# High parts of the projection's input made by ScalarE from the residual stream, and a re-ordered first stage

## What is computed

```python
for l in range(DEPTH):                                  # DEPTH = 2
    cond = silu(c) @ w_ada[l] + b_ada[l]                # 3 x 1024 values
    shift, scale, gate_raw = split(cond, 3)
    h = x * (1.0 + scale) + shift                       # conditioning of the residual stream
    proj = h @ w_in[l]                                  # 33 tiles of 128 columns, and more
    ...                                                 # two scans, merge
    x = layer_norm(DN_ALPHA * x + (1.0 + gate_raw) * out, ln_g[l], ln_b[l])
```

## Time and profile before

| what | value |
|---|---|
| median of three runs | 4421.1 us (4419.56 to 4424.52) |
| the profiled execution's own time | 4417.15 us |
| its span, first to last instruction | 4415.4 us |
| mean granted TensorE clock | 0.919 |
| TensorE busy (weight loads) | 87% (65%) |
| VectorE, ScalarE, GpSimd busy | 53%, 40%, 25% |
| conditioning | 0 to 48.2 us of the span |
| layer 0's projection, first VectorE instruction | 49.03 us |
| layer 1's projection, first VectorE instruction | 1348.48 us |

### The profile page before, as it was taken

How to read it: one execution, slowest core, us unless ns; L and a number is a source line. 1 busy time by engine, 2 the same in 40 slices (tenths; PEclk the granted TensorE clock), 3 DMA queues, 4 the chain that set the end, 5 groups by cost and what they waited for, 6 DMA issues and landing times. The chain is left out here.

```text
span 4415.4 us, 78502 instructions
## 1 busy us (share of the span) xinstructions
PE 3835.2 (87%) x30764; PEld 2891.4 (65%) x30764; DVE 2356.1 (53%) x2943; ACT 1780.8 (40%) x2347; POOL 1097.6 (25%) x963
## 2 busy tenths in 40 slices
PE   6999888888896999978997988888787999999953
PEld 3888676666674887756665754545555777777733
DVE  3365554553663001834554752752356788878857
ACT  1111245442332111444442332542215777777734
POOL 2221213211332221221221320001004444444424
PEclk8999899888998999988988999998798999999975
DMA  6766324112333432333113412511208888898867
GB/s 216 233 223 194 124 86 151 65 51 83 129 100 109 139 124 78 119 117 110 58 44 121 137 67 96 240 41 39 109 38 333 325 305 323 307 391 354 305 219 257
DMA packets 285206, 724.13 MB, mean 164 GB/s; under 512 B 36112, under 2 KB 127888, under 8 KB 268048
## 3 DMA queue, kind: packets, MB, share of 16 engines
q1 hardware_dynamic: 223600, 392.07, 26.0%
q0 software_dynamic: 48960, 283.17, 16.9%
q10 hardware_dynamic: 12384, 45.09, 2.6%
HBM read 631.09 MB, written 168.82 MB: 181 GB/s over the span
## 5 line engine op out<-in xcount | busy, mean ns | idle before, releaser
L471 PE MATMUL ps<-s_proj_hS,s_proj_wS 128*128 128x512 f32 x3216 | 766.7, 401 | 63.2 <-POOL s_proj_wS L361 63.2
L471 PEld LDWEIGHTS ps<-s_proj_hS,s_proj_wS 128*128 128x128 f32 x3216 | 613.7, 191 | 212.2 <-ACT s_proj_wS L421 64.1
L3365 PE MATMUL ps<-s_exp_wS,exp_x 128*128 128x512 f32 x2208 | 539.1, 399 | 0.0
L3365 PEld LDWEIGHTS ps<-s_exp_wS,exp_x 128*128 128x128 f32 x2208 | 408.8, 189 | 92.8
L526 PE MATMUL ps<-gate_h,gate_w 128*128 128x512 f32 x1536 | 417.7, 424 | 37.2 <-PEq L154 19.3
L513 POOL TENSOR_TENSOR gate_w<-gate_raw,gate_w 128x512 fp32r<-128x512 f32 x128 | 187.4, 1467 | 824.0 <-ACT gate_w L507 823.2
L526 PEld LDWEIGHTS ps<-gate_h,gate_w 128*128 128x128 f32 x1536 | 296.0, 197 | 140.2 <-issue 52.1
L389 DVE COPY s_proj_o<-ps 128x512 f32<-128x512 f32 x66 | 45.6, 691 | 567.6 <-PE ps L471 567.6
L3303 DVE TENSOR_TENSOR s_exp_wS<-exp_gu,s_exp_wS 128x1024 fp32r<-128x1024 f32 x276 | 325.3, 1219 | 29.6 <-ACT s_exp_wS L3249 29.6
L361 POOL TENSOR_TENSOR s_proj_wS<-s_proj_w,s_proj_wS 128x1024 fp32r<-128x1024 f32 x67 | 169.0, 2525 | 567.6 <-ACT s_proj_wS L421 567.6
L3249 ACT ACTIVATE s_exp_wS<-exp_gu 128x1024 fp32r<-128x1024 f32 x276 | 286.6, 1071 | 27.0 <-DMA exp_gu<-in_w_gu_dram,s_exp_widx 16.6
(11 more groups left out here) (487 smaller groups left out, 7050.2 us busy)
## 6 DMA issues: line engine op xcount, KB each, us to landing
yrow<-keep_hT SPq DMA_DIRECT2D x92, 512.0 KB, 4.3
keep_mix<-in_w_ada_dram SPq DMA_DIRECT2D x80, 512.0 KB, 7.1
s_proj_w<-in_w_in_dram SPq DMA_DIRECT2D x66, 512.0 KB, 4.3
proj<-s_proj_o ACTq DMA_DIRECT2D x66, 512.0 KB, 2.7
gate_raw<-in_w_in_dram SPq DMA_DIRECT2D x128, 256.0 KB, 3.2
yrow<-keep_xT SPq DMA_DIRECT2D x4, 8192.0 KB, 49.1
s_rw_edge<-proj SPq DMA_DIRECT2D x34, 512.0 KB, 4.9
s_mix_sg<-gates SPq DMA_DIRECT2D x32, 512.0 KB, 3.3
```

Source lines behind the costliest of these rows:

```text
L471: mm = pe.matmul(k.ps[:, 6 + half if last else 2 * b + half, :], wS[:, b, x, t, :], hS[:, y, t, half * HALF:(half + 1) * HALF], start=(t = ...
L3365: mm = pe.matmul(k.ps[:, 2 if u % 2 == 0 else 6, :], xS[:, u % 2, h, 2 * pr + t, :], wS[:, pr, w, t, :], start=(pr == 0 and t == 0 and h + ...
```

## The change

In conditioning, the weights get four buffers, and SP asks for all four groups at once, then for the eight pieces of the residual stream, and waits for these itself at its end; ScalarE issues nothing. The fourth group is no longer multiplied by TensorE against three vectors. VectorE multiplies its rows by the first vector's value of each partition and adds up over the eight slices (`acc`), and TensorE sums over the partitions by products with ones. The bias is added for the first vector alone, which is the only one that this stage's outputs need.

In the projection, ScalarE makes the high part of each piece from `keep_xT` itself, with `1 + scale` and `shift` as scale and bias for each partition. VectorE computes the same piece into `s_proj_o` (two buffers) and makes all eight remainders; GpSimd has none left and begins with the weights. ScalarE makes the first weight tile's high part after the third piece.

```diff
@@ -172,10 +172,11 @@
     NS = 2 * KT
     NG = NS // GRP
     with Stage(k, "ada") as s:
-        w = s.sb("w", [P, 2, GRP, KT, P])
+        w = s.sb("w", [P, NG, GRP, KT, P])
+        acc = s.sb("acc", [P, GRP, P])
         c3, e3 = s.sb("c3", [P, KT, 3]), k.silu
         row = s.sb("row", [3, 2, GRP * P])
-        ld_w, ld_c = [s.sem("ld_w0"), s.sem("ld_w1")], s.sem("ld_c")
+        ld_w, ld_c, ld_x, acc_ready, last_ready = [s.sem(f"ld_w{g}") for g in range(NG)], s.sem("ld_c"), s.sem("ld_x"), s.sem("acc_ready"), s.sem("last_ready")
         sig_ready, silu_ready = s.sem("sig_ready"), s.sem("silu_ready")
         tiles_ready, row_ready, turned, tiles_taken, own = (s.sem(n) for n in "tiles_ready row_ready turned tiles_taken own".split())
         cst, eye_clear = s.sem("cst"), s.sem("eye_clear")
@@ -189,9 +190,10 @@
             sp.dma_start(c3[:], I["c3"]).then_inc(ld_c, 16)
             sp.dma_start(k.bias[:], I["b_ada"]).then_inc(ld_c, 16)
             for g in range(NG):
-                if g >= 2:
-                    sp.wait_ge(tiles_ready, g - 1)
-                sp.dma_start(w[:, g % 2], group(g)).then_inc(ld_w[g % 2], 16)
+                sp.dma_start(w[:, g], group(g)).then_inc(ld_w[g], 16)
+            for t in range(KT):
+                sp.dma_start(k.xT[:, t], I["xT"][t]).then_inc(ld_x, 16)
+            sp.wait_ge(ld_x, 16 * KT)
 
         @block.gpsimd
         def _(pool):
@@ -205,8 +207,6 @@
         def _(act):
             act.wait_ge(ld_c, 32)
             act.activation(e3[:], c3[:], ACT.Sigmoid).then_inc(sig_ready, 1)
-            for t in range(KT):
-                act.dma_start(k.xT[:, t], I["xT"][t]).then_inc(ld_c, 16)
 
         @block.vector
         def _(dve):
@@ -218,16 +218,25 @@
                 dve.tensor_copy(k.cond[:, g * GRP:(g + 1) * GRP, :],
                                 k.ps[:, 2 + g % 2, 0:3 * GRP].rearrange("p (g v) -> p g v", g=GRP)).then_inc(tiles_taken, 1)
 
-            for g in range(NG):
+            for g in range(NG - 1):
                 if g:
                     take(g - 1)
                 dve.wait_ge(tiles_ready, g + 1)
                 dve.tensor_copy(row[:, g % 2], k.ps[0:3, g % 2, :]).then_inc(row_ready, 1)
-            take(NG - 1)
+            dve.wait_ge(ld_w[NG - 1], 16)
+            for t in range(KT):
+                if t:
+                    dve.wait_ge(acc_ready, t)
+                    dve.scalar_tensor_tensor(acc[:], w[:, NG - 1, :, t, :], e3[:, t, 0:1], acc[:], ALU.mult, ALU.add).then_inc(acc_ready, 1)
+                else:
+                    dve.tensor_scalar(acc[:], w[:, NG - 1, :, t, :], e3[:, t, 0:1], None, ALU.mult).then_inc(acc_ready, 1)
+                if t == 2:
+                    take(NG - 2)
+            dve.wait_ge(last_ready, 1)
+            dve.tensor_copy(k.cond[:, (NG - 1) * GRP:NS, 0], k.ps[:, 4, 0:GRP]).then_inc(tiles_taken, 1)
             dve.wait_ge(tiles_taken, NG)
-            dve.wait_ge(ld_c, 32 + 16 * KT)
-            dve.tensor_tensor(k.cond[:, 0:NS], k.cond[:, 0:NS], k.bias[:, 0:NS].unsqueeze(2).to_broadcast([P, NS, 3]),
-                              ALU.add).then_inc(own, 1)
+            dve.wait_ge(ld_c, 32)
+            dve.tensor_tensor(k.cond[:, 0:NS, 0], k.cond[:, 0:NS, 0], k.bias[:, 0:NS], ALU.add).then_inc(own, 1)
 
         @block.tensor
         def _(pe):
@@ -241,18 +250,22 @@
                     tr = pe.transpose(k.ps[:, 2 + g % 2, 3 * x:3 * x + 3], row[:, g % 2, x * P:(x + 1) * P], k.eye[0:3, 0:3])
                 tr.then_inc(turned, 1)
 
-            for g in range(NG):
-                pe.wait_ge(ld_w[g % 2], 16 * (g // 2 + 1))
+            for g in range(NG - 1):
+                pe.wait_ge(ld_w[g], 16)
                 if g == 0:
                     pe.wait_ge(cst, 2)
                 if g >= 2:
                     pe.wait_ge(row_ready, g - 1)
                 for t in range(KT):
-                    mm = pe.matmul(k.ps[0:3, g % 2, :], e3[:, t, :], w[:, g % 2, :, t, :], start=(t == 0), stop=(t == KT - 1))
+                    mm = pe.matmul(k.ps[0:3, g % 2, :], e3[:, t, :], w[:, g, :, t, :], start=(t == 0), stop=(t == KT - 1))
                 mm.then_inc(tiles_ready, 1)
                 if g:
                     turn(g - 1)
-            turn(NG - 1)
+            turn(NG - 2)
+            pe.wait_ge(acc_ready, KT)
+            for x in range(GRP):
+                mm = pe.matmul(k.ps[:, 4, x:x + 1], acc[:, x], k.ones[:, 0:1], start=True, stop=True)
+            mm.then_inc(last_ready, 1)
 
 
 TERMS = ((0, 0), (0, 1), (1, 0))
@@ -280,7 +293,7 @@
         o = s.sb("o", [P, NB, T])
         ld_w = [s.sem(f"ld_w{b}") for b in range(NB)]
         st_o = [s.sem(f"st_o{b}") for b in range(NB)]
-        h_ready, hhi_ready, hlo_v, hlo_p = (s.sem(n) for n in ("h_ready", "hhi_ready", "hlo_v", "hlo_p"))
+        h_ready, hhi_ready, hlo_ready = (s.sem(n) for n in ("h_ready", "hhi_ready", "hlo_ready"))
         hi_ready, lo_ready, half_ready = s.sem("hi_ready"), s.sem("lo_ready"), s.sem("half_ready")
         taken_a, taken_v = s.sem("taken_a"), s.sem("taken_v")
         st_h, st_g, st_x = s.sem("st_h"), s.sem("st_g"), s.sem("st_x")
@@ -337,8 +350,7 @@
                 if 0 <= t < KT:
                     sp.wait_ge(hhi_ready, t + 1)
                     if y:
-                        sp.wait_ge(hlo_v, (t + 1) // 2)
-                        sp.wait_ge(hlo_p, t // 2 + 1)
+                        sp.wait_ge(hlo_ready, t + 1)
                     sp.dma_start(k.scratch["hs"][:, y, t, :], hS[:, y, t, HALF:T].bitcast(F32)).then_inc(st_h, 16)
                     if l and y == 0:
                         sp.dma_start(k.scratch["x1"][t], k.xT[:, t]).then_inc(st_x, 16)
@@ -353,9 +365,6 @@
 
         @block.gpsimd
         def _(pool):
-            for t in range(0, KT, 2):
-                pool.wait_ge(hhi_ready, t + 1)
-                pool.tensor_tensor(hS[:, 1, t], o[:, t % NB], hS[:, 0, t], ALU.subtract).then_inc(hlo_p, 1)
             for i, b, cur, old in steps(pool):
                 wait(pool, hi_ready, i * NB + (b + 1))
                 pool.tensor_tensor(wS[:, b, 1], w[:, b], wS[:, b, 0], ALU.subtract).then_inc(lo_ready, 1)
@@ -366,19 +375,14 @@
             dve.tensor_scalar(sc1[:], k.cond[:, c + KT:c + 2 * KT, 0], 1.0, None, ALU.add).then_inc(h_ready, 1)
             dve.wait_ge(h_ready, 1)
 
-            def low(t):
+            for t in range(KT):
+                if t >= 2:
+                    dve.wait_ge(hlo_ready, t - 1)
+                dve.tensor_scalar(o[:, t % 2], k.xT[:, t], sc1[:, t:t + 1], k.cond[:, c + t, 0:1],
+                                  ALU.mult, ALU.add).then_inc(h_ready, 1)
+                dve.wait_ge(h_ready, t + 2)
                 dve.wait_ge(hhi_ready, t + 1)
-                dve.tensor_tensor(hS[:, 1, t], o[:, t % NB], hS[:, 0, t], ALU.subtract).then_inc(hlo_v, 1)
-
-            for t in range(KT):
-                if t >= NB:
-                    dve.wait_ge(hlo_v, (t - NB + 1) // 2)
-                    dve.wait_ge(hlo_p, (t - NB + 2) // 2)
-                dve.tensor_scalar(o[:, t % NB], k.xT[:, t], sc1[:, t:t + 1], k.cond[:, c + t, 0:1],
-                                  ALU.mult, ALU.add).then_inc(h_ready, 1)
-                if t % 2 == 0 and t:
-                    low(t - 1)
-            low(KT - 1)
+                dve.tensor_tensor(hS[:, 1, t], o[:, t % 2], hS[:, 0, t], ALU.subtract).then_inc(hlo_ready, 1)
             for i, b, cur, old in steps(dve):
                 n = i * NB + b
                 wait(dve, half_ready, n * 2 + 2)
@@ -420,10 +424,12 @@
                 wait(act, half_ready, n * 2 - 2 * NB + 2)
                 act.activation(wS[:, b, 0], w[:, b], ACT.Copy).then_inc(hi_ready, 1)
 
-            high(0, 0)
+            c = l * NADA1
+            act.wait_ge(h_ready, 1)
             for t in range(KT):
-                act.wait_ge(h_ready, t + 2)
-                act.activation(hS[:, 0, t], o[:, t % NB], ACT.Copy).then_inc(hhi_ready, 1)
+                act.activation(hS[:, 0, t], k.xT[:, t], ACT.Identity, scale=sc1[:, t:t + 1], bias=k.cond[:, c + t, 0:1]).then_inc(hhi_ready, 1)
+                if t == 2:
+                    high(0, 0)
             high(0, 1)
             for i, b, cur, old in steps(act):
                 n = i * NB + b
@@ -465,8 +471,7 @@
                     for t in range(KT):
                         if isinstance(n, int) and n == 0 and half == 0:
                             pe.wait_ge(hhi_ready, t + 1)
-                            pe.wait_ge(hlo_v, (t + 1) // 2)
-                            pe.wait_ge(hlo_p, t // 2 + 1)
+                            pe.wait_ge(hlo_ready, t + 1)
                         for x, y in TERMS:
                             mm = pe.matmul(k.ps[:, 6 + half if last else 2 * b + half, :], wS[:, b, x, t, :],
                                            hS[:, y, t, half * HALF:(half + 1) * HALF],
```

## The result

The changed kernel took 4396.95 us in the median of five runs (4395.56 to 4402.04), the kernel before 4421.1 (4417.92 to 4427.19): a ratio of 0.9946, 95% interval 0.9932 to 0.9961. Timed once more beside the other experiments it took 4400.16 against 4420.06, 0.9954 (0.9941 to 0.9967). So the gain is 20 to 24 us, where 16.5 were forecast. The profiled execution is the slowest of the five: 4402.04, span 4400.3, 15.1 less than the profiled execution of before. S and the mark are the prediction's; VectorE's lane is its chain of operations on the eight pieces.

The account below looks back on a forecast made before the run. TensorE's waits at the start of conditioning and of both projections were taken as the bound. Gains of 5.3 (conditioning), 5.1 (layer 0) and 6.1 (layer 1) sum to 16.5: 4421.1 becomes 4404.6, called 4404.5, range 4395 to 4413.

Parts of the forecast that it names:

- S: Start of a layer's projection stage: its first VectorE instruction, at 49.03 us in layer 0 before the change.
- the mark: VectorE's copy of projection step 0's second half; forecast 32.8 us after the stage's start instead of 37.97, layer 1 32.9.
- What bounds it: Projection start: TensorE idles 24.2 us, waiting for GpSimd's first weight remainder; time saved there moves the later steps forward equally.
- Conditioning, 5.3: First stage: all weight groups asked for at once, stream behind them; ends at 42.9 instead of 48.22, bounds 1.5 and 7.
- VectorE's lane, S + 23.7: Projection start: VectorE's eight pieces take 16.4 us, GpSimd's pauses 6.9; last remainder 23.7 after the stage's start, before 25.2.
- ScalarE's price, 1.15 between 1.05 and 1.4: Projection: ScalarE's activation with scale and bias per partition takes 1.15 us, and ScalarE stays ahead of VectorE.
- The second half, 7.7: Projection step 0: TensorE's 24 second-half products take 7.7 us, starting at the low clock and rising; bounds 5.6 and 10.8.
- clock up: Rival, projection: VectorE's bursts keep TensorE warm and GpSimd's pauses cost 1.5 less per layer; 4397.3 us, chance 0.14.
- The sum: Whole kernel: 5.3 + 5.1 + 6.1 = 16.5 us gained; profiled execution 4400.6, median 4404.6.
- the slower case: Rival, conditioning transfers: one queue does not sustain both, decided below 227 GB/s; 1.9 slower or 4428.6 us, chance 0.03.

Follow-up runs that it names:

- x_on_act: Changed kernel with the residual stream's eight transfers issued by ScalarE as before; conditioning ended at 46.70 us instead of 42.41, no whole-kernel time given.
- late_lo: Changed kernel with GpSimd's remainders of the second and third weight tiles held until VectorE's last remainder; 4396.55 us against 4420.57 for the kernel before, 0.9945.
- both_halves: Changed kernel with step 0's products taken piece by piece for both halves, six per piece; 4393.92 us against 4420.57 for the kernel before, 0.9935.
- late_both: Changed kernel with two weight remainders held and step 0's halves taken side by side; 4387.56 us against 4421.6 for the kernel before, 0.9924.
- all_three: Changed kernel with weight remainders held, step 0's halves side by side and VectorE's fourth-group operations earlier; 4379.84 us against 4421.6 for the kernel before, 0.9901.

## Why the prediction was right, and where not

- *What bounds it*: right. TensorE's wait for the first weight remainder was the thing removed, and the mark's gain of 13.16 went through fourteen steps unchanged.
- *Conditioning, 5.3*: it was 5.8 between the first profiles and 4.7 over all. The last byte lands before SP's wait matters, the fourth group's end at 40.1 was forecast at 40.6, and the row scalars were rightly put at nothing. The first group was ready at 9.93, not 9.2, and the first two groups then took 15.80, not 16.8. The size was in part luck: the sum set 6.96 for the third group against an execution in which that group had taken 8.72, so 1.7 of the 5.3 was that execution's clock, which the second profile of before does not have. The reason given, that the gain is the transfers', holds; but that I read it as 1.8 for the first group, with the rest from the missing waits, missed that four buffers alone do not remove these waits: with the stream's queue beside them they stay, as `x_on_act` shows.
- *VectorE's lane, S + 23.7*: S + 22.9. The pieces took 2.0 each, and the three pauses 2.14, 2.03 and 2.04 instead of 2.3. Counted from S the lane ends 2.3 earlier than before (22.9 instead of 25.2). By the rows, four terms make this up, to 0.1. GpSimd's four remainders had held up VectorE by 7.2 in all, and are gone; their four subtractions, with the hand-overs, cost VectorE 5.0. The weight remainders held it up by 0.9 before and by 6.2 now, 5.3 more; and its idle time on ScalarE falls by 5.3, from 5.86 (3.94 + 0.40 + 0.40 + 1.12) to 0.53. The last two cancel, and the prediction named only the first three: it read the whole 25.2 as GpSimd's, though in 3.94 of it VectorE waited for ScalarE, which had the first weight tile to wait for and to copy first. The lines of before that the earlier trace rows leaves out:

```profile
62.98 3.55 DVE L377 TENSOR_SCALAR s_proj_o<-keep_xT,s_proj_sc,keep_cond 128x1024 f32<-128x1024 f32 x2
66.93 1.23 DVE L371 TENSOR_TENSOR s_proj_hS<-s_proj_o,s_proj_hS 128x1024 fp32r<-128x1024 f32 x1 [0.40 <-ACT s_proj_hS L426]
68.07 2.83 DVE L377 TENSOR_SCALAR s_proj_o<-keep_xT,s_proj_sc,keep_cond 128x1024 f32<-128x1024 f32 x1
```

  The Trainium skill (Perfetto Trace Analysis, Optimizing Scalar/DVE Operations) says that moving work between GpSimd and VectorE might not help; by these rows the trace agrees, since the exchange gave back 7.2 for 5.0, but no run makes the exchange by itself.
- *ScalarE's price, 1.15 between 1.05 and 1.4*: the activation with scale and bias per partition took 1.226 (one bias 1.148; without either, 1.046 in the kernel before). It stayed ahead, as said. The Trainium skill (ScalarE: Activation LUTs, What ACT_TABLE_LOAD costs) gives about 93 ns for each such operand; the rows show 102 and 78. No table load came in the projection.
- *The second half, 7.7*: the term that was mis-sized. It took 5.9 in layer 0 at a granted clock of 0.96, and 6.6 in layer 1 at 0.84; the last bursts of three had left TensorE at 0.50, as forecast, but it rose sooner after they ended than I had put it. The rows of the second halves, layer 0 and layer 1 (clock third from the end):

```profile
67.90:73.80 5.90, 5.90 (x26) 4.77 (x25) 0.00 (x0) 0.60 (x1) 0.00 (x0) 0.96 0.00 0
```

```profile
1366.83:1373.40 6.57, 6.57 (x25) 5.23 (x25) 0.00 (x0) 0.59 (x1) 0.00 (x0) 0.84 0.00 0
```

  Of the 2.2 and 1.6 by which the marks came earlier, 1.8 and 1.1 are this term and the rest is the lane's; that is why the marks came at S + 30.59 and S + 31.35 where S + 32.8 and 32.9 stood. The rival "clock up" was nearer in size, but not in its mechanism: it had the bursts themselves keep the clock up. In the changed kernel they did not; bursts of three without pauses between (`late_lo`) and bursts of six (`both_halves`) did.
- *The sum*: 16.5 against 20 to 24 timed and 20.9 between the first profiles at the marks (5.8 + 7.4 + 7.7), 19.0 over all profiles. The profiled execution, forecast at 4400.6, took 4402.04, but by luck: 4.4 more was gained at the marks and 6 lost behind them, 3.1 of these to the clock in steps 1 to 32.
- *The rivals on the other side*: one queue alone moved 2.86 MB in 7 us, 409 GB/s, so the slower case was far off its 227.

## What to carry to other kernels

Where two queues feed one waiting engine, put what is needed later behind what is needed first in the same queue; asking for more at once without that order did nothing here, and with it gave 4.3 us. Before work goes to another engine, ask when that engine is idle: the same eight operations gave nothing at the end of the stage, and 7.9 us when they ran earlier in it. When a chain of small pieces feeds TensorE, give it all the work that each piece allows, and keep GpSimd's operations out of VectorE's chain until it is over (3.5 and 5.9 us at the marks of `late_lo`).

## What the runs showed that was not expected

Identical instructions of one step took 14.86 or 16.39 us, and others 16.4 or 18.0, in steps of about 1.5, as the granted clock fell to its low level in them or not. Over one execution this adds up: steps 1 to 32 took 397.84 or 400.94 in the same kernel, and from there to layer 1 it took 863.6 or 871.7, of which TensorE's longer busy time is 5.6. A single execution of this kernel can be more than 10 us off another (4413.07 to 4435.68 over the runs of before in the last series). The first fourteen steps behind the mark, in which the clock stays up, took 163.89 to 163.91 us in every profile but those of `late_both` and `all_three`, whose step 1 is longer. The stretches before them are less steady: in the kernel before, S moved by 1.9 and the way from S to the mark by 1.0 from one profile to the next. For a change of 20 us in 4400 the marks in the trace, averaged over several profiles, were the sharper instrument, and the whole-kernel times the check on them.
